# An opening that wakes TensorE and takes the constants late, gate products of 16 matmuls, scores behind the products, and a gather buffer cleared by ScalarE

## What is computed

```python
h = rms_norm(x, norm_mix_w)
r_q, r_k, r_v, r_g, m_q, m_k, m_v, m_o, m_i, m_f, gate_r, gate_m = split(h @ w_in)   # 1024 x 8200
# retention, chunk by chunk, R is the state of a head
s = (q @ k.T) * decay_mask
o = s @ v + (q @ R) * q_decay
R = R * chunk_decay + (k * k_decay).T @ v
# mLSTM, the same shape with weights out of the gates m_i + b_i, log_sigmoid(m_f + b_f)
s = (q @ k.T) * exp(dmat - m_t);  h = (s @ v + (q @ C) * w_inter) / max(|den|, exp(-m_t))
C = C * keep + (k * exp(g - m_new)).T @ v
x = x + (sigmoid(gate_r) * (ret @ w_ret) + sigmoid(gate_m) * (hm @ w_mlstm)) @ w_out
# experts: top 1 of 4 groups, top 2 of its 8 experts, each (silu(x @ w_gate) * (x @ w_up)) @ w_down
x = rms_norm(x + moe(rms_norm(x)))
```

## Time and profile before

| What | Value |
|---|---|
| three runs, us | 1064.41 median (1062.72 to 1064.64) |
| the profiled execution's own time, us | 1063.29 |
| its span in the profile, us | 1061.5 |
| TensorE busy | 1004.0 us, 95% |
| VectorE, ScalarE, GpSimd busy | 40%, 26%, 7% |
| moved by DMA | 264.06 MB, mean 249 GB/s |
| granted TensorE clock, mean | 0.987 |

### The profile page before, as it was taken

How to read it: one execution, slowest core, us unless ns; L and a number is a source line. 1 busy time by engine, 2 the same in 40 slices (tenths; PEclk the granted TensorE clock), 3 DMA queues, 4 the chain that set the end, 5 groups by cost and what they waited for, 6 DMA issues and landing times.

```text
span 1061.5 us, 12907 instructions
## 1 busy us (share of the span) xinstructions
PE 1004.0 (95%) x4637; PEld 641.7 (60%) x4637; DVE 425.9 (40%) x733; ACT 277.4 (26%) x464; POOL 70.8 (7%) x102
## 2 busy tenths in 40 slices
PE   4999999999999999999996799999998999998894
PEld 4888888888888888888885333333333433333332
DVE  4237356534543324544525223333332333332236
ACT  6243455443233334622313110000000000000012
POOL 0565000000000000000000000000000000000000
PEclk9999999999999999999998899999999999999998
DMA  7314222222212322206769799999999999999992
GB/s 279 119 40 160 80 80 80 80 80 80 79 51 77 112 80 93 106 14 231 292 272 374 293 420 420 419 420 420 421 419 410 421 420 420 421 416 421 420 415 96
DMA packets 59976, 264.06 MB, mean 249 GB/s; under 512 B 9152, under 2 KB 9216, under 8 KB 35208
## 3 DMA queue, kind: packets, MB, share of 16 engines
q1 hardware_dynamic: 57432, 257.94, 61.8%
q0 software_dynamic: 2480, 5.26, 1.3%
HBM read 263.17 MB, written 4.20 MB: 252 GB/s over the span
## 4 chain that ended last, share of the span: by engine, by line
PE 83%; DMA 12%; DVE 3%; issue 1%; SPq 0%; ACT 0%; DVEq 0%; POOLq 0%; ACTq 0%
PE pj L473 46%; PE pj L671 16%; PE pj L697 8%; DMA raw_moe<-in_w_up_dram 4%; DMA raw_moe<-in_w_down_dram 4%; DMA raw_moe<-in_w_gate_dram 4%; PE cb L439 3%; PE cb L707 2%; PE cb L708 2%; DVE sg L1460 1%; PE cb L492 1%; DMA vrow<-in_mlstm_conv_w_dram 1%; PE cb L518 1%; PE cb L560 1%; PE cb L525 0%
## 5 line engine op out<-in xcount | busy, mean ns | idle before, releaser
L671 PE MATMUL pj<-raw_moe,xT 128*64 128x512 f32 x1024 | 229.4, 598 | 10.9 <-DMA raw_moe<-in_w_up_dram 3.9
L1109 DVE TENSOR_TENSOR wl<-raw_mix,wh 128x1024 fp32r<-128x1024 f32 x88 | 109.5, 1249 | 182.5 <-ACT wh L844 182.3
L671 PEld LDWEIGHTS pj<-raw_moe,xT 128*64 128x64 f32 x1024 | 73.5, 137 | 150.7 <-issue 150.6
L473 PE MATMUL pj<-wh,hTh 128*128 128x512 f32 x320 | 129.9, 406 | 1.6 <-DVE hTl L1137 1.6
L473 PE MATMUL pj<-wl,hTh 128*128 128x512 f32 x320 | 125.2, 391 | 0.0
L473 PE MATMUL pj<-wh,hTl 128*128 128x512 f32 x320 | 124.9, 390 | 0.0
L844 ACT ACTIVATE wh<-raw_mix 128x1024 fp32r<-128x1024 f32 x88 | 92.5, 1057 | 122.4 <-PE pj L473 110.8
L697 PE MATMUL pj<-raw_moe,hf 128*64 128x512 f32 x512 | 116.7, 598 | 0.8 <-ACT hf L1058 0.8
L1444 DVE TENSOR_TENSOR x<-x,cb 128x512 f32<-128x512 f32 x120 | 76.9, 683 | 99.2 <-PE cb L708 99.2
L473 PE MATMUL pj<-hTh,wh 128*128 128x512 f32 x192 | 80.0, 417 | 0.0
L473 PE MATMUL pj<-hTh,wl 128*128 128x512 f32 x192 | 75.4, 393 | 0.0
(11 more groups left out here) (280 smaller groups left out, 1207.2 us busy)
## 6 DMA issues: line engine op xcount, KB each, us to landing
raw_moe<-in_w_gate_dram SPq DMA_DIRECT2D x64, 1024.0 KB, 9.6
raw_moe<-in_w_up_dram SPq DMA_DIRECT2D x64, 1024.0 KB, 10.2
raw_moe<-in_w_down_dram SPq DMA_DIRECT2D x64, 1024.0 KB, 9.7
raw_mix<-in_w_in_dram SPq DMA_DIRECT2D x32, 1024.0 KB, 5.1
raw_mix<-in_w_ret_branch_dram SPq DMA_DIRECT2D x4, 1024.0 KB, 5.1
raw_mix<-in_w_mlstm_branch_dram SPq DMA_DIRECT2D x4, 1024.0 KB, 5.7
raw_mix<-in_w_out_dram SPq DMA_DIRECT2D x4, 1024.0 KB, 5.2
xt<-in_x_dram SPq DMA_DIRECT2D x4, 512.0 KB, 4.8
```

What stands on the lines that cost most here:

```text
L473: m = nc.tensor.matmul(pj[:, i, :], lhsT, rhs, start=k == 0 and n == 0, stop=k == KD - 1 and n == 2)
L671: mm = nc.tensor.matmul(pj[a * CAP:(a + 1) * CAP, up, :], xT[:, 4 * half + k, a * CAP:(a + 1) * CAP], raw_moe[(m + a) % MOE_RAW][:, k, :], ...
L1109: V.tensor_tensor(wl[:, q % RING, :, :], raw_mix[n % MIX_RAW][:, 2 * (q % 2):2 * (q % 2) + 2, :], wh[:, q % RING, :, :].bitcast(F32), ALU. ...
```

## The change

It has six parts. (1) SyncE loads only the identity (128 columns of `kc`) ahead of the vectors and the weight chunks; the rest of the constants and the gate weights follow the first three chunks, and nothing waits for the turned vectors. (2) TensorE first multiplies a tile of ones by itself 22 times into a part of `pj` that is overwritten later. (3) The norm's factor is made for two tiles, then for the other two; VectorE scales all four, ScalarE copies the turned vectors, and they are turned between the second and the third tile. The second weight tail comes after the fourth `hTl`, the third head after the sixth `hTh`. (4) The tails of the gate weights go into columns 64 to 67 and 96 to 99 of `wgh`, so that two sums (`hTh`, `hTl`) of 8 matmuls are enough; the four row groups are read out in `B_RK` and added by VectorE. With this the product tail x tail is summed too. (5) Scores of the next head are issued right behind the products of this one; in the last chunk of the mLSTM the keys are no longer turned or weighted. (6) ScalarE clears `xg` with a scale of 0 before the exponents of the routing.

```diff
-            sp.dma_start(kc[:, :], consts[:, 0:K_SELH]).then_inc(c_in, 16)
-            sp.dma_start(selh[:, :], consts[0:H, K_SELH:K_END]).then_inc(c_in, 16)
+            sp.dma_start(kc[:, K_IDENT:K_IDENT + P], consts[:, K_IDENT:K_IDENT + P]).then_inc(id_in, 16)
...
             for n in range(MIX_RAW):
                 mix_chunk(n)
-            sp.wait_ge(vT, 1)
+            sp.dma_start(kc[:, K_RMASK:K_SELH], consts[:, K_RMASK:K_SELH]).then_inc(c_in, 16)
+            sp.dma_start(kc[:, 0:K_IDENT], consts[:, 0:K_IDENT]).then_inc(c_in, 16)
+            sp.dma_start(selh[:, :], consts[0:H, K_SELH:K_END]).then_inc(c_in, 16)
...
-            pe.wait_ge(c_in, 32)
-            pe.wait_ge(v_in, 80)
-            turn(cb[:, 3, 0:64], vrow[:, :], 64).then_inc(vT, 1)
+            def wake(n):
+
+                for _ in range(n):
+                    nc.tensor.matmul(pj[:, 0, (TT - 1) * P:T], onesq[:, :], onesq[:, :], start=True, stop=True)
+
+            pe.wait_ge(zero_ok, 1)
+            wake(WAKE)
+            pe.wait_ge(id_in, 16)
             for t in range(TT):
-                pe.wait_ge(xs_ok[t % 2], t // 2 + 1)
-                if t == 0:
+                if t == 2:
+                    pe.wait_ge(v_in, 80)
+                    turn(cb[:, 3, T - 64:T], vrow[:, :], 64).then_inc(vT, 1)
+                pe.wait_ge(xs_ok, t + 1)
+                if t == 2:
                     pe.wait_ge(vC, 1)
...
-                turn(cb[:, 2 + i % 2, 0:P], mkT[:, h, cs]).then_inc(m_s, 1)
+                m = nc.tensor.matmul(cb[:, i % 2, 0:P], mkT[:, h, cs], mqT[:, h, cs], start=True, stop=True)
+                if c < TT - 1:
+                    m = turn(cb[:, 2 + i % 2, 0:P], mkT[:, h, cs])
+                m.then_inc(m_s, 1)
...
-                        for n, (w_, a_) in enumerate(((wgh, hTh), (wgh, hTl), (wgl, hTh))):
+                        for n, a_ in enumerate((hTh, hTl)):
...
-                    if B_MQ <= b < B_RG:
-                        ret_scores(b - B_MQ, j)
-                    if B_RG <= b < B_GM:
-                        ml_scores(b - B_RG, j)
+                    if b == B_MQ and j == 0:
+                        ret_scores(0)
+                    if b == B_RG and j == 0:
+                        ml_scores(0)
...
                         ret_products(b - B_MQ, j)
+                        if 4 * (b - B_MQ) + j < 15:
+                            ret_scores(4 * (b - B_MQ) + j + 1)
                     if B_RG <= b < B_GM:
                         ml_products(b - B_RG, j)
+                        if 4 * (b - B_RG) + j < 15:
+                            ml_scores(4 * (b - B_RG) + j + 1)
...
                 nc.scalar.activation(rvo[:, t, :], xt[:, t, :], ACT.Square, accum_out=ssq[:, t:t + 1]).then_inc(sq_ok, 1)
-            root(0, TT)
-            act.wait_ge(v_own, RSTD_STEPS)
-            for t in (1, 3):
-                nc.scalar.activation(xs0[:, t, :], xt[:, t, :], ACT.Copy, scale=stat[:, 2, t:t + 1]).then_inc(xs_ok[1], 1)
+                if t == 1:
+                    root(0, 2)
+            root(1, 2, 2)
+            act.wait_ge(vT, 1)
+            nc.scalar.activation(vcol[:, :], cb[:, 3, T - 64:T], ACT.Copy).then_inc(vC, 1)
             mix_head(0)
             mix_head(1)
...
+                    if b == B_RK and j == 1:
+                        act.wait_ge(g_ps, 1)
+                        nc.scalar.activation(grow[:, 1, :], cb[32:32 + H, 3, :], ACT.Copy).then_inc(grow_a, 1)
+                        nc.scalar.activation(grow[:, 3, :], cb[96:96 + H, 3, :], ACT.Copy).then_inc(grow_a, 1)
...
+            nc.scalar.activation(xg[:, :], onesq[:, 0:1].to_broadcast([P, D]), ACT.Copy, scale=0.0).then_inc(zero_ok, 1)
             act.wait_ge(e1_in, 1)
...
-            rstd(0, ssq[:, 0:TT], TT, D)
-            for t in (0, 2):
-                V.tensor_scalar(xs0[:, t, :], xt[:, t, :], stat[:, 2, t:t + 1], None, ALU.mult).then_inc(xs_ok[0], 1)
+            for u in range(2):
+                dve.wait_ge(sq_ok, 2 * u + 2)
+                rstd(u, ssq[:, 2 * u:2 * u + 2], 2, D, 2 * u)
+                for t in (2 * u, 2 * u + 1):
+                    V.tensor_scalar(xs0[:, t, :], xt[:, t, :], stat[:, 2, t:t + 1], None, ALU.mult).then_inc(xs_ok, 1)
...
-            pool.wait_ge(lg_ps, 2)
-            pool.memset(xg[:, :], 0.0).then_inc(zero_ok, 1)
```

More of the change, by code:

```diff
@@ L63 @@
 LEAD = RING - 1
-RSTD_STEPS = 5
+WAKE = 22
 MIX_RAW = 3
@@ L235, in hybrid_block @@
         x_in = [sem(f"x_in{t}") for t in range(TT)]
+        id_in = sem("identity_in")
         raw_in = [sem(f"raw_in{s}") for s in range(MIX_RAW)]
@@ L244, in hybrid_block @@
         vT, vC, zero_ok = sem("vectors_turned"), sem("vector_columns"), sem("memsets")
-        xs_ok = [sem("x_scaled_even"), sem("x_scaled_odd")]
+        xs_ok = sem("x_scaled")
         at_ok = sem("slots_ready")
@@ L477, in mix_half, with ret_scores @@
                         m.then_inc(pair_used, 1)
-            def ret_scores(c, h):
-                i, cs = 4 * c + h, slice(c * P, (c + 1) * P)
+            def ret_scores(i):
+                c, h = divmod(i, 4)
+                cs = slice(c * P, (c + 1) * P)
                 if i == 0:
@@ L500, in ret_products, with ml_scores @@
                 m.then_inc(r_o, 1)
-            def ml_scores(c, h):
-                i, cs = 4 * c + h, slice(c * P, (c + 1) * P)
+            def ml_scores(i):
+                c, h = divmod(i, 4)
+                cs = slice(c * P, (c + 1) * P)
                 if i == 0:
@@ L558, in _ @@
                     for k in range(KD):
-                        for n, (w_, a_) in enumerate(((wgh, hTh), (wgh, hTl), (wgl, hTh))):
-                            m = nc.tensor.matmul(cb[:, 3, :], w_[:, k, :], a_[:, k, :], start=k == 0 and n == 0, stop=k == KD - 1 and n == 2)
+                        for n, a_ in enumerate((hTh, hTl)):
+                            m = nc.tensor.matmul(cb[:, 3, :], wgh[:, k, :], a_[:, k, :], start=k == 0 and n == 0, stop=k == KD - 1 and n == 1)
                     m.then_inc(g_ps, 1)
@@ L593, in _ @@
                         if j == 3:
-                            pe.wait_ge(grow_a, 2)
+                            pe.wait_ge(grow_a, 4)
                         for h in range(H):
@@ L867, in _ @@
                 nc.scalar.activation(hTh[:, k, :], (pj, cb)[k // 4][:, k % 4, :], ACT.Identity, scale=vcol[:, k:k + 1]).then_inc(hTh_ok, 1)
-                if k == 4:
+                if k == 5:
                     mix_head(2)
@@ L961, in _ @@
                     ret_output(15)
-                    root(1, 16)
+                    root(2, 16)
                 for j in range(4):
@@ L972, in _ @@
                         mix_head(q + LEAD)
+                    if b == B_RK and j == 1:
+                        act.wait_ge(g_ps, 1)
+                        nc.scalar.activation(grow[:, 1, :], cb[32:32 + H, 3, :], ACT.Copy).then_inc(grow_a, 1)
+                        nc.scalar.activation(grow[:, 3, :], cb[96:96 + H, 3, :], ACT.Copy).then_inc(grow_a, 1)
+                    if b == B_RK and j == 2:
+                        nc.scalar.activation(grow[:, 0, :], cb[0:H, 3, :], ACT.Identity, bias=bif[:, 0:1]).then_inc(grow_a, 1)
+                        nc.scalar.activation(grow[:, 4, :], cb[64:64 + H, 3, :], ACT.Copy).then_inc(grow_a, 1)
                     if b == B_RV + 1:
@@ L1018, in _ @@
                     if b in (B_MO + 1, B_MO + 2) and j == 2:
-                        root(2 + b - B_MO - 1, 8)
+                        root(3 + b - B_MO - 1, 8)
             def square(t):
@@ L1040, in _ @@
             stream_copy(3)
-            root(4, TT)
+            root(5, TT)
             for u in range(2):
@@ L1090, in _ @@
                 final_square(2 * u + 1)
-                root(5 + u, 2, 2 * u)
+                root(6 + u, 2, 2 * u)
         @block.vector
@@ L1276, in _ @@
                 if b == B_RV:
-                    dve.wait_ge(grow_a, 2)
-                    own(V.tensor_scalar(grow[:, 1, :], grow[:, 1, :], bif[:, 1:2], None, ALU.add))
+                    dve.wait_ge(grow_a, 4)
+                    own(V.scalar_tensor_tensor(grow[:, 1, :], grow[:, 1, :], bif[:, 1:2], grow[:, 3, :], ALU.add, ALU.add))
                     V.scalar_tensor_tensor(grow[:, 2, :], grow[:, 1, :], -1.0, grow[:, 1, :], ALU.mult, ALU.max).then_inc(f_abs, 1)
+                    own(V.tensor_tensor(grow[:, 0, :], grow[:, 0, :], grow[:, 4, :], ALU.add))
                 if b == B_RG:
                     dve.wait_ge(r_out, 16)
-                    rstd(1, ssq[:, :], 16, DV)
+                    rstd(2, ssq[:, :], 16, DV)
                     own(V.tensor_copy(rret[:, :], stat[:, 2, :]))
@@ L1353, in _ @@
                         dve.wait_ge(sq_ok, TT * (2 + half))
-                        rstd(2 + half, ssq[:, 8 * half:8 * half + 8], 8, DV)
+                        rstd(3 + half, ssq[:, 8 * half:8 * half + 8], 8, DV)
                         for t in range(TT):
@@ L1368, in _ @@
             dve.wait_ge(sq_ok, 4 * TT)
```

(6 more changed lines are left out.)

25 lines of the change are left out of this document (7 added, 18 removed).

## The result

The changed kernel takes 1056.21 us in the median of four runs (1055.12 to 1056.24), the kernel before 1063.93 in four. The ratio is 0.9926 (95% interval 0.9909 to 0.9943), that is 7.9 us less, with 6 to 9.7 in the interval; between the two medians it is 7.7. The four executions are 1055.12, 1056.20, 1056.22 and 1056.24.

What follows compares the result with a forecast made beforehand. The expert weights' DMA stream, tied to TensorE's first expert products, was taken to bound the end. Terms 4.6 + 1.9 + 1.5 + 0.4 + 0.6 = 9.0 off 1063.29 give 1054.3, with half a microsecond for the runs 1054.8; range 1052.6 to 1057.9.

Steps and rivals of the forecast that it cites:

- the clock rival: Opening: TensorE's clock falls back and the stream starts at 1.2 GHz, 2.2 us less won, so 1057.0; chance 0.2.
- The opening, -4.6: Before the mixer's stream: `hTh` starts at 13.5 and not 18.08, the stream at 15.8; -4.6 us (-3.4 to -5.1).
- the small DMAs for the vectors may hold the queue: Opening: part of the rival that the chunk lands later or breaks don't merge; 1.2 to 2.7 us less, chance 0.15.
- The norm's chain: Opening: squares, scaled tiles and transposes ahead of `hTh`, which by this chain could start at 13.0 us.
- stream matmuls 0.43 apart at the start: Start of the mixer's stream: a spacing in us named as a sign that the prediction is wrong.
- The gates, -1.9: Gate matmuls on TensorE: eight fewer than 24, at 0.233 us each; -1.9 us.
- The scores, -1.5: Mixer's stream: 30 of 32 scores move next to products, 30 breaks go at about 0.05 us each; -1.5 us.
- The turns, -0.4: Last mLSTM chunk: four turns of keys less, 0.11 us each; -0.4 us.
- the clearing, -0.6: Routing: without GpSimd's clearing of the gather buffer, VectorE's first operations speed up; -0.6 us (0 to -0.9).
- The first pair: First expert pair on TensorE: 32 matmuls take 8.41 us at a varying clock; 1 us allowed both ways.
- nothing arrives at the end: Expert weights: their stream is bound by its own start in the mixer and ends where it did, 1064; chance 0.04.
- slower: Mixer steps: scores behind the products wait for the copy of the output before, in 30 steps, up to 1070; chance 0.03.

Runs made afterwards that it cites:

- consts_early: The changed kernel with all constants loaded ahead of the vectors and the first weight chunk again; 1059.77 us, ratio 0.9958 to the kernel before.
- changed_again: The changed kernel timed a second time, nothing changed; 1055.96 us in the median of five, ratio 0.9929 to the kernel before.
- changed_third: The changed kernel timed a third time, nothing changed; 1056.27 us, ratio 0.9926 to the kernel before.
- gpsimd_clears: The changed kernel with xg cleared by GpSimd again; 1056.21 us, ratio 0.9930 to the kernel before.
- awake_routing: The changed kernel with products of ones on TensorE through the routing (29, 8 and 25); 1054.82 us, 1.14 less than the changed kernel.
- awake_opening: The changed kernel with products of ones in the opening's gaps alone, none around the routing; 1055.24 us, 1.03 less than the changed kernel beside it.
- no_wake: The changed kernel without the 22 products of ones; 1055.70 us, ratio 0.9925 to the kernel before.
- awake_both_again: Second timing of the changed kernel with products of ones in the opening's gaps and around the routing; 1053.41 us, ratio 0.9903 to the kernel before.

## Why the prediction was right, and where it was off

The direction, the time within its range (1056.21 in 1052.6 to 1057.9) and most terms came out. The median is 1.4 above the forecast of 1054.8 and nearer to the 1057.0 of the clock rival, and by the two groups three of the result's four executions are of the kind that this rival describes, though the one that has a trace is not among them. The sum of 9.0 was 0.8 too high against the spans of the two profiles. That this profile shows the clock up through the whole opening was luck.

*What bounds the kernel.* Right: the first expert product moved by 8.42 us and the span by 8.2, and no wait of TensorE came up between the opening and the routing. (In the earlier trace rows the slices at 410 to 421 GB/s are 16 in a row and not 15; nothing rests on it.)

*The opening, -4.6.* Measured -4.15. The chain was the right one (`consts_early` puts 2.06 us of it back), its size a little too large: the chunk was in use at 12.03 and not 11.5, and at 12.38 and 12.01 in the other two profiles of the changed kernel. That the small DMAs for the vectors may hold the queue was a rival; no run moved them, so it stays open. The norm's chain came out later as well, at about 13.65 instead of 13.0: the third square started at 7.67, having waited for its token tile. In `changed_again` and `changed_third` it started at 7.10 and 7.04; there the last tile was turned from 12.71 and 12.65 on, so this chain was ready at about 13.0, as reckoned, a microsecond ahead of the other.

*The clock.* This is the step that failed. "Against it that the clock was up at 17.7 and stayed so over the 1.6 us gap ahead of 20.36": with this I gave the low clock 0.2 and a price of 2.2 us. What failed is the reading that a clock which had stayed up over one gap would stay up over the new one. Four of six profiles of versions with this opening and its 22 ones have the fall, with 23.5 to 23.7 us for the 96 matmuls (`changed_again`, `gpsimd_clears`, `awake_routing`, `changed_third`), two have not (22.05, 22.04); the executions of the changed kernel fall in two groups some 1.6 us apart, and the gaps filled with ones (`awake_opening`) take away the upper group. The gap before was 1.6 us and came after six microseconds of transposes; the new one is 1.82 to 2.80 us and comes after the last sixteen of them, 1.8 us by their spacing, where the prediction had 0.9. The sign named for this rival, stream matmuls 0.43 apart at the start, stands in those four profiles. The price was 1.6 us and not 2.2. By the Trainium skill ("TensorE: Matmul & The Clock Gate", Part 4: PE-mode transpose) transposes don't count as activity as matmuls do; `no_wake` has the clock rise at about 12.3 us with nothing but transposes of the opening ahead of it, so in this kernel they do.

*The 22 ones.* I had taken from "with TensorE awake the last eight transposes need 0.9 us" that they were a part of the gain. `no_wake` shows no loss in time that can be measured without them: the stream started 0.95 us later there, and the clock did not fall.

*The gates, -1.9.* Measured -1.87, by the two traces; no run undoes it.

*The scores, -1.5.* Measured 1.39 in the sum and 1.49 in the run that undoes it: the cause, the disturbed matmuls around a break, is shown.

*The turns, -0.4, and the clearing, -0.6.* The turns are gone from the program, and nothing measured them by themselves; the clearing is 0.63 by the run that undoes it.

*The first pair.* I allowed 1 us both ways; in three profiles of the changed kernel the 32 matmuls took 7.98, 8.30 and 8.58.

Of the rivals, "nothing arrives at the end" and "slower" fall with the same rows: the shift at the first expert product arrives, and no step waits for a copy.

## What to carry to other kernels

Products that only wake TensorE are worth nothing if it then runs out of work before the stretch that needs the clock: look at the busy time of the stretch just ahead of it, and fill the gaps up to it, in a part of PSUM that is free or overwritten later. A short burst of other matmuls in a long stream costs some 0.05 us in its neighbours beside its own time, so bursts go together. And ask of a transfer in front what else stands in the same queue: here a megabyte of constants cost three to four microseconds, two of them by the wait alone and the rest by the clock that fell in it. A chain that is made shorter than the one it meets only lengthens a wait: here the earlier transposes went with the lost clock.

## What the runs showed of the hardware

A single profile can be of the better of two groups. The same program kept its clock up from its first rise on through the opening in one execution (22.05 us for 96 matmuls) and had it down for 3.4 us in another (23.65). The engines ran the same instructions, but not at the same times: the token tiles came at different moments, and TensorE's wait ahead of the stream was 1.82 us in the one and 2.49 in the other. The clock rose between 4.9 and 7.0 us in the executions that began with ones.

The wait just ahead of a fall in the opening was 2.49 to 3.68 us, the longest that was not followed by one 2.28. From 13.40 to 16.80 TensorE had 0.91 us of work in `changed_third`, where the clock fell, 3.27 in `awake_both_again`, where it didn't, and in the first profile of the changed kernel, where it didn't either, 1.58:

```profile
13.40:16.80 3.40, 1.58 (x13) 1.28 (x11) 3.17 (x5) 3.40 (x7) 0.00 (x0) 1.00 1.06 394
```

In the middle of the experts, between 801 and 815 us, TensorE stands still for 3.1 to 3.8 us in every version, with no wait that the profile shows. In the changed kernel and most versions the clock falls behind it; in the kernel before and in `consts_early` it didn't. 48 matmuls take 12.22 us there in the changed kernel and 10.52 before; first the changed kernel, then the kernel before:

```profile
806.75 12.22 PE L689 MATMUL pj<-raw_moe,xT 128*64 128x512 f32 x48 [3.60 <-issue]
```

```profile
814.49 10.52 PE L671 MATMUL pj<-raw_moe,xT 128*64 128x512 f32 x48 [3.08 <-issue]
```

It may not be free. In the 4 us around it (802 to 806) the DMAs of the changed kernel move 352 and 348 GB/s, where they otherwise move about 420; in the kernel before it is 363 and 338 (810 to 814). Both kernels show it, so it doesn't bear on the comparison, but at this place `awake_routing` loses 0.6 us of its lead. The cause is open; no run moved it.
